# Expert rows fetched per pair instead of per group, in a two-block transformer kernel on one Trainium2 core

## The reference

```
def hier_moe(h, w_grp, b_grp, w_rtr, b_rtr, w1, w3, w2):
    t = h.reshape(-1, d)
    grp_prob = jax.nn.softmax((t @ w_grp).astype(F32) + b_grp, axis=-1)
    g_prob, g_sel = lax.top_k(grp_prob, 1)
    exp_logits = ((t @ w_rtr).astype(F32) + b_rtr).reshape(-1, N_GROUPS, EXP_PER_GROUP)
    in_grp = jnp.take_along_axis(exp_logits, g_sel[:, :, None], axis=1)[:, 0]
    e_prob, e_sel = lax.top_k(jax.nn.softmax(in_grp, axis=-1), TOP_K_IN_GROUP)
    gate = g_prob * e_prob / jnp.sum(e_prob, -1, keepdims=True)
    ...
    hid = jax.nn.silu(jnp.einsum('td,edf->tef', t, w1)) * jnp.einsum('td,edf->tef', t, w3)
    y = jnp.einsum('tef,efd->td', hid * combine[..., None].astype(hid.dtype), w2)
```

## Time and profile before

| | us |
|---|---|
| median of three runs | 1307.88 |
| lowest and highest run | 1305.73, 1312.74 |
| span of the profiled execution | 1303.9 |
| PE busy in it | 1269.3 |
| DVE, ACT, POOL busy | 559.9, 486.9, 115.5 |

### The profile page before, as it was taken

One profiled execution on the slowest core, in us unless ns is written; L12 is line 12 of the kernel. 1 busy time (PEld: TensorE's weight loads), 2 busy tenths in 40 slices (PEclk: granted clock), 3 DMA queues, 4 the chain that ended last, 5 costly groups with the idle time before them and its releaser, 6 DMA issues.

```text
span 1303.9 us, 19404 instructions
## 1 busy us (share of the span) xinstructions
PE 1269.3 (97%) x7567; PEld 815.6 (63%) x7567; DVE 559.9 (43%) x1226; ACT 486.9 (37%) x1066; POOL 115.5 (9%) x167
## 2 busy tenths in 40 slices
PE   9999999999999999999999998999999999999996
PEld 7888588885787877454344443788877554444432
DVE  3335223262676584342232215678485342222224
ACT  3346343462753245212223323663235312223232
POOL 0000000000014321000000000004322000000000
PEclk9999999999999999979999999999999999999998
DMA  9753162332521124749999999231132859999994
GB/s 367 150 179 112 50 268 97 130 111 78 205 98 67 66 98 172 308 170 377 420 420 420 422 416 407 100 113 67 66 130 99 341 213 397 419 421 420 422 420 195
DMA packets 48848, 307.40 MB, mean 236 GB/s; under 512 B 5897, under 2 KB 6409, under 8 KB 16752
## 3 DMA queue, kind: packets, MB, share of 16 engines
q1 hardware_dynamic: 43760, 288.61, 56.0%
q0 software_dynamic: 3200, 8.16, 2.8%
q10 hardware_dynamic: 1792, 9.31, 1.9%
HBM read 301.05 MB, written 8.59 MB: 237 GB/s over the span
## 4 chain that ended last, share of the span: by engine, by line
PE 80%; DVE 13%; ACT 5%; issue 2%; DMA 1%; ACTq 0%; DVEq 0%; SPq 0%
PE ps L1150 22%; PE ps L1840 18%; PE ps L1867 9%; PE ps L1417 4%; PE ps L1190 4%; PE ps L1909 2%; PE ps L1930 2%; PE ps L1118 2%; DVE projT L2792 1%; DVE small L2791 1%; PE ps L1158 1%; PE ps L1649 1%; PE ps L1849 1%; DVE projT L2783 1%; PE ps L1540 1%
## 5 line engine op out<-in xcount | busy, mean ns | idle before, releaser
L1150 PE MATMUL ps<-hT,ring 128*128 128x272 f32 (+1 forms) x1760 | 416.8, 390 | 0.6 <-ACT hT L2027 0.6
L1150 PEld LDWEIGHTS ps<-hT,ring 128*128 128x128 f32 x1760 | 327.1, 190 | 62.6 <-issue 7.0
L1840 PE MATMUL ps<-ring,arena 128*64 128x512 f32 x416 | 139.4, 600 | 0.0
L3157 DVE TENSOR_TENSOR xo<-ps,xo 128x512 fp32r<-128x512 f32 x64 | 42.9, 689 | 99.3 <-ACT xo L2465 99.3
L3278 POOL TENSOR_TENSOR arena<-projT,cst 32x272 f32<-32x272 f32 x104 | 71.6, 689 | 114.1 <-DVE projT L2770 101.0
L1840 PE MATMUL ps<-projT,arena 128*64 128x512 f32 x240 | 80.0, 597 | 0.0
L3148 DVE TENSOR_TENSOR arena<-arena,ps 128x256 f32<-128x256 f32 x32 | 13.5, 422 | 140.0 <-ACT arena L2452 139.4
L1840 PEld LDWEIGHTS ps<-ring,arena 128*64 128x64 f32 x416 | 40.1, 137 | 52.0 <-issue 51.2
L2450 ACT ACTIVATE arena<-ps 128x256 f32<-128x256 f32 x32 | 12.3, 386 | 138.7 <-PE ps L1840 138.7
L1417 PE MATMUL ps<-ring,projT 128*128 128x512 f32 x128 | 56.6, 596 | 0.0
L1190 PE MATMUL ps<-ring,arena 128*128 128x512 f32 x128 | 55.9, 593 | 0.0
(11 more groups left out here) (518 smaller groups left out, 2045.8 us busy)
## 6 DMA issues: line engine op xcount, KB each, us to landing
ring<-experts SPq DMA_DIRECT2D x72, 1024.0 KB, 16.2
ring<-w_in SPq DMA_DIRECT2D x62, 1024.0 KB, 5.4
projT<-experts SPq DMA_DIRECT2D x48, 1024.0 KB, 15.6
arena<-experts SPq DMA_DIRECT2D x22, 1024.0 KB, 12.8
prm<-experts SPq DMA_DIRECT2D x22, 1024.0 KB, 15.9
ring<-w_out SPq DMA_DIRECT2D x16, 1024.0 KB, 4.8
spare<-experts SPq DMA_DIRECT2D x12, 1024.0 KB, 14.5
lent<-experts SPq DMA_DIRECT2D x8, 1024.0 KB, 10.1
```

Source lines behind the costliest of these rows:

```text
L1150: mm = pe.matmul(ps[:, chunk_bank(blk, l, j), 0:ncols], w[:, j % 2, k, :], hT[:, k, T - ncols:T], start=(k == 0), stop=(k == KC - 1))
L1840: mm = pe.matmul(ps[64 * e:64 * e + 64, 0, :], xg[:, 4 * h + k, i % 2, 64 * e:64 * e + 64], w[e][:, k // 2, 512 * (k % 2):512 * (k % 2) + ...
L3157: v.tensor_tensor(low, ps[:, 4 + half, :], high, ALU.subtract).then_inc(s("pair_rows_copied"), 1)
```

## The change

- Rows of groups 1 to 3 are no longer fetched per group. After `gates_in(g)` VectorE computes a token index for each slot (`slot_tokens`), and GpSimd issues one indirect DMA of 128 rows per pair (12 a layer) into one of three buffers (`pair_rows`). Each waits until the one before has landed.
- VectorE turns such a pair's rows into the layout that the matmuls want, with 16 transposes of 32 x 256 (`turn_tokens`). TensorE's `gather_two` and ScalarE's copies remain for pairs 2 and 3 alone.
- The first group's rows are not fetched at all. TensorE makes them in the router stage (`first_rows`, from `res` with `xsel`, two halves), in the place of `first_tokens` and of `keep_busy`. ScalarE copies them to `xrows`. SP's wait for the first fetch is gone, and so are VectorE's index for it (L3028) and the memset of `xrows`.
- `turn_group(g + 1)`, `select_pairs(g + 1)` and `gates_in(g + 1)` move from the third to the first pair of group g, so those of group 1 stand in iteration 0. `gate_slots(1)` stands at the end of iteration 0, the others two pairs earlier than before. `psel` has a second buffer in `hT`, where `xselT` lies too, so the slot `lent` stays in use to the end of the stage.

```diff
-LAST_USE = {LENT: 57, ONCE[1]: 75, CONSTS_ROOM: 79, NORMS_ROOM: 79}
+LAST_USE = {ONCE[1]: 75, CONSTS_ROOM: 79, NORMS_ROOM: 79}
+SLOT_FACTS = 2 * PER_GROUP + 1
...
                         sp.wait_ge(layer_normed, normed_at[l, 1, 2, 1])
-                        sp.wait_ge(rows_fetched, 16 * (GROUPS * l + 1))
...
-                def first_tokens():
+                def first_rows(half):
                     pe.wait_ge(s("group_selected"), 1)
                     for t in tiles:
                         n = ROWS[t]
-                        mm = pe.matmul(ps[:, 2, 0:2], xsel[0:n, t, :], const("row_codes")[0:n, 2 * t:2 * t + 2],
+                        mm = pe.matmul(ps[:, 3 * half, :], xsel[0:n, t, :], res[0:n, t, 512 * half:512 * half + 512],
                                        start=(t == t0), stop=(t == 2))
...
                 keep_busy(5, 448)
-                first_tokens()
-                keep_busy(5, 512, 512, 512)
+                first_rows(0)
+                if l == LAYERS - 1:
+                    first_rows(1)
...
-                    pe.wait_ge(s("pair_tokens_copied"), copies_of(i) - (h == 0))
+                    if i < PAIRS_A_GROUP:
+                        pe.wait_ge(s("pair_tokens_copied"), copies_of(i) - (h == 0))
+                    else:
+                        pe.wait_ge(s("row_places"), places_left(i))
...
-                        if q == 2 and g + 1 < GROUPS:
+                        if q == 0 and g + 1 < GROUPS:
                             turn_group(g + 1)
                         up_half(i, 1)
-                        if i % 2 and i + 1 < PAIRS:
-                            gather_two(i + 1, 0)
+                        if i == 1:
+                            gather_two(2, 0)
                         if i:
                             down(i - 1)
                         if i == 0:
                             gate_slots(0)
                             gather_pair(1)
-                        elif i % 2 and i + 1 < PAIRS:
-                            gather_two(i + 1, 1)
+                            gate_slots(1)
+                        if i == 1:
+                            gather_two(2, 1)
...
                 turn_group(0)
-                keep_busy(4, *([256] if l < LAYERS - 1 else [384, 512, 512, 384]))
+                if l < LAYERS - 1:
+                    first_rows(1)
+                else:
+                    keep_busy(4, 384, 512, 512, 384)
...
+                    for half in range(2):
+                        a.wait_ge(s("group_rows_done"), half + 1)
+                        L(a.activation(xrows[:, 512 * half:512 * half + 512], ps[:, 3 * half, :], ACT.Copy), s("group_rows_copied"))
...
                     v.wait_ge(s("pair_gates_done"), g + 1)
+                    if g:
+                        facts = ps[:, 5, 32:32 + SLOT_FACTS * PAIRS_A_GROUP].rearrange("p (q n) -> p q n", n=SLOT_FACTS)
+                        VP(v.tensor_scalar(slot_tokens[:, g % 2, :], facts[:, :, SLOT_FACTS - 1], -0.5, float(NO_ROW - T // 2),
+                                           ALU.mult, ALU.add))
...
+                def turn_tokens(i):
+                    v.wait_ge(rows_fetched, fetched_by(l, i))
+                    v.wait_ge(up_used, 2 * PAIRS * l + 2 * (i - 2) + 2)
+                    rows = pair_rows[(i - PAIRS_A_GROUP) % 3].rearrange("p (k j r) -> p k j r", j=4, r=32)
+                    for j in range(4):
+                        for slots in range(4):
+                            here = slice(32 * slots, 32 * slots + 32)
+                            ins = v.transpose(xg[32 * j:32 * j + 32, :, i % 2, here], rows[here, :, j, :])
+                    ins.then_inc(s("row_places"), 1)
...
-                        if q == 2 and g + 1 < GROUPS:
+                        if q == 0 and g + 1 < GROUPS:
                             select_pairs(g + 1)
                             gates_in(g + 1)
-                        if q == 3 and g + 1 < GROUPS:
-                            split_rows(g + 1)
                         hidden(i)
...
+                        if i + 2 in turned_pairs():
+                            turn_tokens(i + 2)
...
-                for group in range(GROUPS):
-                    g.wait_ge(s("group_tokens_ready"), group + 1)
...
+                for i in turned_pairs():
+                    group, q = i // PAIRS_A_GROUP, i % PAIRS_A_GROUP
+                    g.wait_ge(s("pair_gates_copied"), group + 1)
+                    g.wait_ge(s("row_places"), 1 if i == PAIRS_A_GROUP else max(3, places_left(i - 3)))
+                    if fetched_by(l, i - 1):
+                        g.wait_ge(rows_fetched, fetched_by(l, i - 1))
+                    g.indirect_dma_start(pair_rows[(i - PAIRS_A_GROUP) % 3], None, normed_rows,
+                                         bass.IndirectOffsetOnAxis(ap=slot_tokens[:, group % 2, q:q + 1], axis=0),
+                                         bounds_check=T - 1, oob_is_err=False).then_inc(rows_fetched, 16)
```

More of the change, by code:

```diff
@@ L629, in late_by, with turned_pairs, fetched_by, places_left @@
             return 16 + 16 * (l + 1) + 16 * min(l + 1, LAYERS - 1)
+        def turned_pairs():
+            return range(PAIRS_A_GROUP, PAIRS)
+        def fetched_by(l, i):
+            return 16 * ((PAIRS - PAIRS_A_GROUP) * l + i - PAIRS_A_GROUP + 1)
+        def places_left(i):
+            return i - PAIRS_A_GROUP + 4
         def head_banks(b, t):
@@ L839, in program @@
         xrows, ax = more(ax, D)
-        xplaces, ax = more(ax, 3 * PER_GROUP)
-        psel = halved("psel", ax, PER_GROUP, EXPERT_SLOTS)[:, :, :]
+        xplaces, ax = more(ax, 4 * PER_GROUP)
+        psels = [halved("psel", ax, PER_GROUP, EXPERT_SLOTS)[:, :, :],
+                 nc.alloc_sbuf_tensor_at("psel_odd", [P, PER_GROUP, EXPERT_SLOTS], F32R, offset=hT_at + 4 * D)[:, :, :]]
+        xselT = hT.rearrange("p k n -> p (k n)")[:, D + PER_GROUP * EXPERT_SLOTS:D + PER_GROUP * EXPERT_SLOTS + T]
+        assert D + PER_GROUP * EXPERT_SLOTS + T <= KC * T
         ax += PER_GROUP * EXPERT_SLOTS
@@ L1857, in down @@
                         pe.wait_ge(s("pair_rows_copied"), 2 * i)
-                    if i % PAIRS_A_GROUP == 1 and i + PAIRS_A_GROUP < PAIRS:
-                        gate_slots(i // PAIRS_A_GROUP + 1)
-                    if i == PAIRS_A_GROUP * (GROUPS - 2) + 1:
+                    before = i % PAIRS_A_GROUP == PAIRS_A_GROUP - 1 and i + 1 < PAIRS_A_GROUP * (GROUPS - 1)
+                    if before:
+                        gate_slots(i // PAIRS_A_GROUP + 2)
+                    if i == PAIRS_A_GROUP * (GROUPS - 2) - 1:
                         pe.wait_ge(s("group_turned_copied"), 1)
                     for half in range(2):
-                        if half == 1 and (i == 0 or i % PAIRS_A_GROUP == 1 and i + PAIRS_A_GROUP < PAIRS):
-                            pe.wait_ge(s("pair_gates_copied"), 1 if i == 0 else i // PAIRS_A_GROUP + 2)
+                        if half == 1 and (i == 0 or before):
+                            pe.wait_ge(s("pair_gates_copied"), 2 if i == 0 else i // PAIRS_A_GROUP + 3)
                         for f in range(2):
@@ L1876, in gate_slots @@
                     for q in range(PAIRS_A_GROUP):
[L1877 to L1878 removed]
+                        mm = pe.matmul(ps[:, 5, 32 + SLOT_FACTS * q:32 + SLOT_FACTS * (q + 1)],
+                                       whole(psels[g % 2])[:, 2 * q:2 * q + 2, :], xplaces[:, PER_GROUP:PER_GROUP + SLOT_FACTS],
+                                       start=True, stop=True)
                     mm.then_inc(s("pair_gates_done"), 1)
@@ L1909, in gather_two @@
                             mm = pe.matmul(ps[:, 2 + k // 2, (k % 2) * 2 * P:(k % 2 + 1) * 2 * P], rows[:, c],
-                                           psel[:, 2 * q:2 * q + 4, :], start=(part == 0), stop=(part == 1))
+                                           psels[0][:, 2 * q:2 * q + 4, :], start=(part == 0), stop=(part == 1))
                     mm.then_inc(s("pair_gathered"), 1)
@@ L2483, in experts_grouped @@
                                 hidden_in(i - 1)
-                            if q == 2 and g + 2 == GROUPS:
+                            if q == 0 and g + 2 == GROUPS:
                                 turned_in()
@@ L2488, in experts_grouped @@
                             gate_sigmoid(i)
-                            if i == 0 or i % 2 and i + 1 < PAIRS:
+                            if i < 2:
                                 tokens_in(i + 1)
@@ L3257, in send @@
             def send(l, group):
+                g.wait_ge(s("group_tokens_ready"), group + 1)
                 g.wait_ge(s("group_sums_copied"), 2 * group + 2)
```

90 lines of the change are left out of this document (46 added, 44 removed).

## The result

The changed kernel takes 1326.87 us (median of 4 runs, 1325.19 to 1332.56) against 1308.93 for the kernel before (4 runs, 1305.73 to 1312.74): ratio 1.0158, 95% interval 1.0139 to 1.0177. It is slower, as forecast, and 6 us slower than the 1321 of the forecast. The profiled execution took 1325.19 us, its span is 1323.4 against 1303.9: 19.5 us more.

What follows compares the result with a forecast made beforehand. The weights' DMA stream was taken to set the stages' end, with TensorE nearly as close. Layers of 6.4 us each gave 12.8 on the 1303.9 span, 1316.7; the median lies 4.0 above, so 1321 us, range 1310 to 1332.

Steps and rivals of the forecast that it cites:

- parts 1, 2, 5: Six of seven gathers a layer gone, SP's first-fetch wait gone, VectorE's transposes added: all hidden, 0 us each.
- part 3: Iteration 0 gets longer by group 1's work, delaying the slots: 4.2 us in layer 0, 3.2 in layer 1.
- part 4: More rows through the same DMA engines, 12 fetches a layer for 3: 3.2 us a layer, ends 0 and 11.7.
- part 6: Start of layer 0's stage: 1 us sooner, ends 3 sooner and 2 later; layer 1: 0.
- The bound: Expert stages end when the last weights land, so TensorE's saved gathers turn into waits for weights, worth 0.
- Rival a: TensorE is the bound after all and weights come sooner: 17 us faster, 1291 us; chance 0.08.
- rival c: Weight waits or VectorE cost more than hidden, or the clock falls late in the stage: about 1338 us; chance 0.10.
- Part 5: VectorE's 16 transposes a pair take 5.5 us (4.3 to 6.7), within 7.1 us of room: cost 0.
- The signs named: Half-gathers 28 to 4, TensorE idle in pairs 9 to 15, layer 1 gate-to-pair-1 about 12 us, last items 5 to 8 later.

Runs made afterwards that it cites:

- b_high_only: The kernel before with only the high part in `gather_two`, half of the gathers' matmuls left out: 1305.78 us.
- b_first_rows: The kernel before with group 0's rows made by TensorE in the router stage, without their fetch and SP's wait; groups 1 to 3 fetched as before: 1310.76 us.
- ai_less_dma: a_iter1 with a quarter of each of layer 1's weight items not loaded from item 30 on: 1293.97 us.
- less_dma: Quarter of each layer 1 weight item not loaded from item 30 on: kernel before 1304.37 us, changed kernel 1308.77, a_iter1 1293.97.
- a_iter1: The changed kernel with group 1's work moved from iteration 0 to iteration 1: 1315.16 us.
- b_delay: The kernel before with seven matmuls of 128x512 that compute nothing at the end of iteration 0 of each layer: 1324.22 us.
- a_busy: The changed kernel with matmuls that compute nothing in iteration 0, one ahead of `turn_group(1)` and two behind `gate_slots(1)`: 1323.49 us.
- ai_spread: a_iter1 with another order of an expert's slots, meant to spread the fetched rows over the DMA engines: 1312.78 us.
- a_no_fetch: The changed kernel with layer 1's twelve fetches of pairs 4 to 15 left out: 1324.18 us.

## Why the prediction was right, and 6 us short

| step of the prediction | forecast, us | measured, us |
|---|---|---|
| parts 1, 2, 5: gathers, SP's wait, transposes | 0 | 0 (b_high_only -1.9, b_first_rows +2.7, ai_less_dma) |
| part 3, layer 0 | 4.2 (5.4 less 1.2) | 5.8 |
| part 3, layer 1 | 3.2 (4.7 less 1.5) | 8.0, of them 3.4 clock |
| part 4, layer 0 and 1 | 3.2 and 3.2 | 2.7 and 3.5 |
| part 6, layer 0 | -1.0 | -0.5 |
| sum | 12.8 | 19.5, span difference 19.5 |

Part 3 is `up(1, 1)` of the changed kernel less that of b_first_rows, which differs from it ahead of that point by iteration 0 alone. Part 4 is the length less `up(1, 1)`, changed kernel less the kernel before. Part 6 is the start of the stage, 0.6 later, with `up(1, 1)` of b_first_rows, 1.0 sooner. The differences are taken before rounding, and all are of single profiles, so each is good to 1 or 1.5 us.

- **The bound.** Right. The gathers fell from 28 half-gathers to 4, TensorE's idle time grew by 15.5 and 16.7 us a layer behind the first 25 us, with the DMA share at 1.01 and 0.98. Rival a is refuted by b_high_only; the less_dma kernels show that its 13.8 us a layer exist and lie under the weights.
- **Part 3, the mis-sized term.** Its mechanism, iteration 0 delays the slots, was right: a_iter1 takes most of it away and gives 11.7 us back. What TensorE needs longer was right as well: 5.4 and 4.7 forecast, 5.8 and, without the clock, 4.6 measured. Two things were wrong. The stream was to take up 1.2 and 1.5 us of it; it takes up nothing (b_delay, 5.6 and 5.9 us in, 5.9 and 6.3 out). And the clock was put at nothing here: rival c expected falls of the clock late in the stage, from waits for weights. They came there as well (0.89 over 780 to 795 us, 0.86 over 1280 to 1292), at times when TensorE waits for weights anyway. The ones that cost 3.4 us (a_busy) are those behind the two waits that part 3 itself added in iteration 0, where TensorE sets the pace of the stream. The Trainium skill (TensorE: Matmul & The Clock Gate, HAM oscillation — how this bites in real kernels) was cited for the late waits. It tells of longer waits, all for DMA; this trace agrees that waits lower the clock, but shows it behind waits for VectorE of only 1.2 and 1.8 us (0.72 and 0.84), and that place was missed.
- **Part 4.** Right in size, 2.7 and 3.5 for 3.2, though the upper end of 11.7 was far off. A single pair of landings 3.8 us apart was no measure for twelve smaller fetches. The rows' bytes alone are less: the queue moved 1.8 MB more than in b_first_rows (9.58 for 7.78), 4.3 us at 417 GB/s over both layers, where parts 4 come to 6.2. ai_spread takes 1.8 and 1.2 us away by moving the rows among partitions, which fits an engine that has most; the margin is small. The Trainium skill's rule (DMA: Bandwidth & Descriptors, The descriptor swizzle), which the forecast set at 0.8 us a layer, agrees with that in direction.
- **The range.** That 1326.87 lies within 1310 to 1332 is in part luck. Part 3 passed its own upper ends, 5.8 for 5.4 and 8.0 for 4.7, and the room for it came from the end of 11.7 of part 4, which was too high.
- **Part 5.** The transposes take 7.0 us a pair, just above the upper bound of 6.7 and within the room of 7.1. VectorE's busy time grew by 153.6 us (forecast 130) at hardly a price: even where the weights set no bound, TensorE waited 1.6 us for it behind iteration 0 (ai_less_dma).
- **Part 6.** The stage of layer 0 started 0.6 us later than before, not 1.0 sooner; over all these profiles the start lies between 580.8 and 584.4, so the sign of that isn't shown. But the first half "up" then takes 3.65 us for 4.69, in every kernel with `first_rows`: 1 us, as much as the forecast took. It had named a lift of the clock by a fuller TensorE as possible; the granted clock of the first 25 us is 0.96 for 0.88, which fits.
- **The signs named.** Pair 1's first matmul follows the gate step by 13.3 us (1081.79 to 1095.13), 12 were forecast, 7.1 before; the last items came 7.5 and 11.5 us late, for 5 to 8.

Open: what makes the clock fall in iteration 0 of layer 0 in some executions and not in others, how much of a_no_fetch's 2.7 to 6 us is the fetches, and why b_first_rows is 2.7 us slower in the median when its profile is not. By the medians a_iter1 is only some 5 us above b_first_rows, where the profiles of the two differ by 8 us in both layers together.

## What to carry to other kernels

When weights stream through a ring of slots, look at when the first slots come free before counting what an engine saves later. Here every microsecond by which they came free late was paid in full at the end, and work taken from the middle was worth nothing while the stream was as long. A low DMA share in the first microseconds of the stage hints at it, but compare it with a kernel that has as many items in before the stage: in layer 1, 0.71 came with 0.6 us more and 0.50 with 11.5. Put bookkeeping for later groups behind the first slots' release, even at the same total work. And where two engines hand work to and fro in that stretch, count the waits twice: once as time, and once as the clock that TensorE may lose in them.

## What the runs showed of the hardware

- Behind waits of TensorE of 1.2 and 1.8 us in iteration 0 the granted clock fell to 0.72 and 0.84 over 6 and 11 us, so to the lower of its two levels (1.2 GHz) for a part of them (two blocks of 16 matmuls took 5.28 and 5.35 us instead of 3.58). With one and two matmuls of 512 columns that compute nothing in those waits the blocks took 3.58 and 3.62 us, and the total was 3.4 us less.
- Such falls are not the same in each execution: in layer 0 one of three profiles of the same code had none (`up(1, 1)` at 21.2), two had them (24.4 and 25.9).
- A VectorE transpose of 32 x 256 f32 takes 435 ns, as long as an arithmetic operation on 128 x 256 (421 ns in before), though it covers a quarter of the partitions.
- Twelve indirect fetches of rows of 4 KB in the place of three larger ones, beside a full stream of weights, cost 2.7 and 3.5 us a layer. With the rows on other partitions the layers were 1.8 and 1.2 us shorter, near the spread between executions.
- TensorE at 12.6 or 13.6 us a pair makes no difference to the end of the stage while six items of 1 MB take 15.
- In layer 0, `up(1, 1)` came between 15.4 and 25.9 us over the twelve executions without ai_spread, and what followed differed by no more than 1.4 us among kernels with the same kind of fetch: nothing of a delay was caught up.
